# A two-block network on one core: the gating bias in two passes for both token blocks, and products of ones between bare attention steps

## What is computed

```python
def spatial_gating(h, w_in, ln_g, ln_b, w_s, b_s, w_out):
    u, v = jnp.split(jax.nn.gelu(h @ w_in), 2, axis=-1)          # 2048 wide each
    v = layer_norm(v, ln_g, ln_b)
    vg = v.reshape(B, nc, SG_CHUNK, SG_GROUPS, SG_WIDTH // SG_GROUPS)   # 2 blocks of 128 tokens, 8 groups
    mixed = jnp.einsum('gts,bcsgd->bctgd', w_s, vg) + b_s.T[None, None, :, :, None]
    return (u * mixed.reshape(B, L, SG_WIDTH)) @ w_out

def odd_mixer(x, w_in, q_norm_g, kv_norm_g, w_uq, w_ukv, w_o):
    out_c = dsa_attention(...)            # 8 heads, each token sees its 64 best-scored keys
    out_d = causal_block_attention(...)   # 8 heads
    return jnp.concatenate([out_c, out_d], axis=-1) @ w_o
```

## Time and profile before

| | |
|---|---|
| median of three runs | 2561.55 us |
| the profiled execution | 2558.21 us, its span 2556.4 us |
| mean granted TensorE clock | 0.968 |
| TensorE busy | 2424.2 us, 95% of the span |
| VectorE busy | 1718.7 us, 67% |
| ScalarE busy | 1191.6 us, 47% |
| DMA | 501 MB, 196 GB/s on average |

### The profile page before, as it was taken

How to read it: one execution, slowest core, us unless ns; L and a number is a source line. 1 busy time by engine, 2 the same in 40 slices (tenths; PEclk the granted TensorE clock), 3 DMA queues, 4 the chain that set the end, 5 groups by cost and what they waited for, 6 DMA issues and landing times.

```text
span 2556.4 us, 34122 instructions
## 1 busy us (share of the span) xinstructions
PE 2424.2 (95%) x14294; PEld 2078.5 (81%) x14294; DVE 1718.7 (67%) x2273; ACT 1191.6 (47%) x1523; POOL 98.9 (4%) x187
## 2 busy tenths in 40 slices
PE   7999999898989999999999999989999899899997
PEld 3778888667789999998899997767777777678776
DVE  5997776653766656655556655577887684678776
ACT  3222222333554544446344444465766644566665
POOL 0111111010000000000000000000000000000000
PEclk9999999999999999999899999999999996999999
DMA  6777787322124545465245542257887521388774
GB/s 274 231 238 263 264 265 252 132 79 94 67 100 167 184 178 179 168 224 191 105 149 177 189 174 102 99 184 271 335 323 293 211 94 53 138 309 329 295 289 175
DMA packets 80386, 501.16 MB, mean 196 GB/s; under 512 B 9605, under 2 KB 10709, under 8 KB 28497
## 3 DMA queue, kind: packets, MB, share of 16 engines
q1 hardware_dynamic: 59120, 423.66, 45.1%
q0 software_dynamic: 21088, 75.01, 9.2%
HBM read 497.58 MB, written 1.05 MB: 195 GB/s over the span
## 4 chain that ended last, share of the span: by engine, by line
PE 70%; DVE 16%; ACT 9%; issue 3%; DMA 2%; ACTq 0%; DVEq 0%; SPq 0%
PE bank L402 68%; DVE wl L1957 7%; ACT wh L1340 6%; DVE macc L1993 1%; ACT s L1438 1%; DVE f L2152 1%; PE bank L613 1%; DVE s L2143 1%; DVE rs L2017 1%; PE bank L1234 1%; DMA raw<-in_wstream 1%; DMA raw<-in_wmod 1%; DMA mring<-in_wmod 1%; DVE hl L2127 0%; ACT H L1447 0%
## 5 line engine op out<-in xcount | busy, mean ns | idle before, releaser
L1957 DVE TENSOR_TENSOR wl<-raw,wh 128x2048 fp32r<-128x2048 f32 (+1 forms) x432 | 903.8, 2097 | 410.7 <-ACT wh L1340 407.8
L1340 ACT ACTIVATE wh<-raw 128x2048 fp32r<-128x2048 f32 (+1 forms) x432 | 755.3, 1756 | 365.2 <-PE bank L402 349.3
L402 PE MATMUL bank<-hh,wh 128*128 128x258 f32 (+2 forms) x2200 | 696.6, 317 | 31.6 <-DVE wl L1957 7.7
L402 PE MATMUL bank<-hh,wl 128*128 128x258 f32 (+2 forms) x2200 | 676.8, 308 | 0.0
L402 PE MATMUL bank<-hl,wh 128*128 128x258 f32 (+2 forms) x2200 | 675.4, 307 | 0.0
L402 PEld LDWEIGHTS bank<-hh,wh 128*128 128x128 f32 x2200 | 424.2, 193 | 62.0 <-DVE hl L2127 8.1
L402 PEld LDWEIGHTS bank<-hl,wh 128*128 128x128 f32 x2200 | 424.8, 193 | 18.5
L402 PEld LDWEIGHTS bank<-hh,wl 128*128 128x128 f32 x2200 | 422.8, 192 | 18.9
L402 PE MATMUL bank<-wh,hh 128*128 128x512 f32 (+1 forms) x704 | 277.9, 395 | 5.5 <-DVE hl L2903 2.8
L402 PE MATMUL bank<-wh,hl 128*128 128x512 f32 (+1 forms) x704 | 273.4, 388 | 0.0
L402 PE MATMUL bank<-wl,hh 128*128 128x512 f32 (+1 forms) x704 | 273.3, 388 | 0.0
(11 more groups left out here) (437 smaller groups left out, 2678.1 us busy)
## 6 DMA issues: line engine op xcount, KB each, us to landing
raw<-in_wstream SPq DMA_DIRECT2D x393, 1024.0 KB, 4.9
mring<-in_wmod POOLq DMA_DIRECT2D x128, 512.0 KB, 4.6
raw<-in_wmod SPq DMA_DIRECT2D x6, 1024.0 KB, 7.1
X<-in_xT SPq DMA_DIRECT2D x1, 2048.0 KB, 12.4
mods<-in_wmod SPq DMA_DIRECT2D x2, 1024.0 KB, 18.9
bias<-in_nabias POOLq DMA_DIRECT2D x16, 128.0 KB, 2.5
c_sglg<-in_sglg POOLq DMA_DIRECT2D x1, 1024.0 KB, 4.5
c_sglb<-in_sglb POOLq DMA_DIRECT2D x1, 1024.0 KB, 6.6
```

The source lines that it names most:

```text
L402: return e.matmul(out, lhsT, rhs, start=start, stop=stop, skip_group_check=True)
L1340: e.activation(wh[i % NB][:, o], raw[i % NR][:, o], ACT.Copy).then_inc(*slab_high(st.split + m))
L1957: e.tensor_tensor(wl[i % NB][:, o], raw[i % NR][:, o], wh[i % NB][:, o].bitcast(F32), ALU.subtract).then_inc(*slab_low(st.split + m))
```

## The change

In `gating(m)` the bias comes first and is added for both token blocks at once: two fp32r products of one row, whose moving operand is the group's 128 biases repeated twice by a zero step, once with the high part `sg.bh` and once with the low part `sg.bl`. Then follow the two f32 products with `sg.ws`, accumulating. ScalarE writes `sg.bh` (1024 values in one partition) and `sg.one` (128 ones) before it evacuates the first quarter of v; VectorE writes `sg.bl` as the difference ahead of v's sums. `sg.bh` takes the place of `sg.tmp` in memory, which is dead by then.

A helper `fill(n, cols)` issues n f32 products of the 128x128 `ones` with `ones` to the bank that is next in turn, without claiming it; nobody reads the result. `fill(2, P)` comes behind each of the five bare steps and behind each `turned(i)`, seven times in all, 14 products of 128 columns.

```diff
@@ sg room @@
-        sg.tmp = sb(ph, "tmps", [P, 4, T])
+        with ExitStack() as pre:
+            sg.tmp = sb(pre, "tmps", [P, 4, T])
+        sg.bh = sb(ph, "sgbh", [1, 8 * P], F32R)
...
+        sg.bl = sb(ph, "sgbl", [1, 8 * P], F32R)
+        sg.one = sb(ph, "sgone", [1, P], F32R)
@@ TensorE @@
+        def fill(n, cols=T):
+            b = st.turn % 8
+            while b in st.kept:
+                b = (b + 1) % 8
+            if b in st.drain:
+                w.wait_ge(*st.drain[b])
+            w.wait_ge(dve_out, "ones")
+            out = banks[b][:, 0:cols].rearrange("p (a b) -> p a b", b=P)
+            for _ in range(n):
+                mm(out, ones[:], ones[:].unsqueeze(1).to_broadcast([P, cols // P, P]), True, True)
...
                 w.wait_ge(dve_out, "v norm")
                 w.wait_ge(const_in["sgws"], 0)
-                w.wait_ge(const_in["sgbs"], 0)
+                w.wait_ge(act_out, "sg one")
+                w.wait_ge(dve_out, "sg bias")
+                for t, first in ((sg.bh, True), (sg.bl, False)):
+                    mm(b[:, 0:T].rearrange("p (q t) -> p q t", q=2), sg.one[:], t[:, P * g:P * g + P].unsqueeze(1).to_broadcast([1, 2, P]),
+                       first, False)
                 for q in range(2):
-                    mm(b[:, P * q:P * q + P], sg.v[:, q, P * m:P * m + P], sg.ws[:, g, :], True, False)
-                    ins = mm(b[:, P * q:P * q + P], ones[0:1, :], sg.bs[:, P * g:P * g + P], False, True)
+                    ins = mm(b[:, P * q:P * q + P], sg.v[:, q, P * m:P * m + P], sg.ws[:, g, :], False, True)
...
-            attend(5)
+            for _ in range(5):
+                attend(1)
+                fill(2, P)
             for i in (2, 3):
                 turned(i, bank(("turn", "od", i), dve_out, "turn l", "od", i))
+                fill(2, P)
                 attend(1)
@@ ScalarE, quarter n of v @@
                 w.wait_ge(result, "sgv", n)
+                if n == 0:
+                    w.wait_ge(const_in["sgbs"], 0)
+                    e.activation(sg.bh[:], sg.bs[:], ACT.Copy).then_inc(*act_out("sg bias"))
+                    e.activation(sg.one[:], ones[0:1, :], ACT.Copy).then_inc(*act_out("sg one"))
@@ VectorE, layer_norms @@
                 mean, var = (sg.st[:, :, i] for i in (4, 5))
+                w.wait_ge(act_out, "sg bias")
+                e.tensor_tensor(sg.bl[:], sg.bs[:], sg.bh[:].bitcast(F32), ALU.subtract).then_inc(*dve_out("sg bias"))
```

## The result

The changed kernel took 2550.6 us (median of 22 executions, 2524.2 to 2593.0), the kernel before 2570.2 us (22 executions, 2551.2 to 2615.5). The ratio is 0.9908, 95% interval 0.9883 to 0.9933, so it is faster by 24 us (17 to 30). The prediction said 2526 and 2517 to 2546: the direction was right, the time lay 4.6 us above the range, and the gain was a third smaller than the 35.5 us forecast.

A forecast was written before the change was run, and what follows sets the result against it. TensorE's order of work was taken to bound the kernel. Gating 18.0 plus mixer 17.5 gave 35.5 us off the profiled 2558.2, so 2522.7; with 3.3 for the median of three runs, 2526 us, range 2517 to 2546.

The forecast's parts named there:

- 18.0 us forecast: Gating: shorter bias products and full clock in both blocks of four save 18.0 us, about 9 of it the clock.
- Rival C: Each gating's two bias products: the repeated operand is read slowly, at 1.2 us each; 2574 us, slower; chance 0.05.
- Rival A: Gating's blocks of four: the low clock stays once or twice, 4.6 us each; 2531 to 2535 us; chance 0.13.
- The mixer's sum: Second mixer: bare steps save 0.8 us and the stretch after them 16.7 us, together 17.5 us.
- The bare stretch: Second mixer's bare attention steps, 2108.51 to 2124.15: 15.6 us becomes 14.8 at full clock, fills included; saves 0.8.
- which one fill shortens to about 0.3: Second mixer, before 2119.16: one fill cuts TensorE's 0.78 us wait for Y to about 0.3 us.
- The stretch behind: Second mixer, 2124.15 to 2161.39: 37.2 us at half clock becomes 20.5 at full clock; saves 16.7 us.
- VectorE is busy only 14.9 us of those 37.2 and ScalarE 12.8 ... so both fit: Second mixer after the bare steps: both engines' busy times fit into the 20.5 us forecast there.
- Rival B: Second mixer: the clock falls despite the fills, about +4 us instead of -17.5; 2547 us; chance 0.11.
- For it ... one fall at any of the seven steps lasts to 2161: Second mixer, argument for Rival B: a single clock fall at any filled step keeps the clock low until 2161.
- Its own scatter is that of the three runs, 6 us each way: Whole kernel: the forecast time scatters 6 us each way, as the three runs of the kernel before did.
- I read the recurrence as evidence that such a mixture holds the clock: From 683.40 to 710.70, four-row and full-height f32 products kept 1.00 for 27.3 us; so new gating blocks likely would.

## Why the prediction was off

**The gating was right term by term.** 18.0 us forecast, 18.0 found, in all nine traces of the new form. A gating is 1.06 to 1.07 us against 1.07; VectorE's subtraction is 1.21 us against 1.2 and takes all of the slack, with 0.15 us of waiting on ScalarE and at most 0.1 us on v, where I took 0; ScalarE's two passes 1.35 against 1.4; the wait for z 0.37 against 0.3. Within it two prices offset each other: a one-row product with the repeated operand costs 0.20 us rather than 0.12, and seems to include the change of height that I had counted by itself (the two passes together 0.42 us, against 0.24 and one change of 0.19). Rival C, that such an operand is slow, is out. Rival A, that the low clock stays, is out: no new gating ever fell. In the one-row fills' trace TensorE was busy in 7.20 of 7.20 us and fell to 0.50. The Trainium skill, "TensorE: Matmul & The Clock Gate", section "Why this matters for your kernels", says that a TensorE kept busy without gaps keeps its clock; that trace disagrees.

**The mixer's sum was 3 us too high.** 17.5 us forecast, 14.5 in the best case, 1.5 short in each half. The bare stretch was to go from 15.6 to 14.8 us and became 16.3 (2091.57 to 2107.83), because a fill costs 0.60 us behind 64-column products (0.45 taken; the switch to other heights around it was left out), and because the two waits in it are 0.66 and 0.85 us where 0.3 was put. The step "which one fill shortens to about 0.3" failed: with the clock up, TensorE comes to Y sooner, and VectorE does not finish it sooner. In the two traces whose bare steps ran with fills at 0.50 there is no wait before Y's first turn. The stretch behind was to take 20.5 us and took about 22, 1.12 of it the next wait for Y. "VectorE is busy only 14.9 us of those 37.2 and ScalarE 12.8 ... so both fit" is the step there: a small busy share does not say that a result is ready when it is wanted. The prediction's list of what could go wrong had a wait for exp, not one for Y or hl, and the sum had no term for it.

**The mixer's clock was treated as certain or absent.** The forecast had one fall, at the bare steps, that the fills cure, and B had it stay. "For it ... one fall at any of the seven steps lasts to 2161" looked at the seven steps alone. The traces show a third thing: the bare steps hold under full-height fills, and the clock falls at another wait, behind Y (13.7 us in three of four traces of the changed kernel), behind hl, or 57 us ahead of the first fill. With three of four at 78.2 instead of 72.0 us this is an estimated 4.7 us of the mean. 35.5 - 3.0 - 4.7 gives 27.8, inside the measured 17 to 30. Rival B's 2547 is the nearest of the times forecast, by luck: it had the mixer gain nothing, and in the changed kernel's four traces the mixer gained 8.3 or 14.5 us.

**The base was too low, and its scatter too small.** "Its own scatter is that of the three runs, 6 us each way" is the step that failed here. The median of the kernel before beside the result was 2570.2, 8.6 above the 2561.55 of the three runs; the mean over the 86 is 2574.0, and single executions go 40 us further. Either miss alone would have left the time in the range: 2561.6 less the measured 24 is 2538, and 2570.2 less the forecast 35.5 is 2535. Together they put it outside. A base of 2574.0 less 27.8 is 2546; measured are medians around 2551, mean 2552.4. Three runs were few. But the trace itself could have warned: with 20 separate stretches at 0.50, and a recurrence that runs 4-row and 128-row products in turn and happened to stay at 1.00, much in one execution is chance. I read the recurrence as evidence that such a mixture holds the clock. In seven of twelve traces it didn't.

**What stays open.** The two traces lose 61 us at 0.50 between them (163 to 102), the means only 40 (206 to 166), and the difference of the means of the times is 21.6 (2.6) us, 6 less than the 27.8, more than two standard errors. The trace after was as much a favourable execution of its kernel as the first trace was of its own. Where the other executions have the rest of their low time can't be seen, since only profiled ones show it. One place is known: the mixer of the fills-alone trace, which has the same TensorE program there, took 102.3 us. Counted in, the five mixers with the seven fills are 9.8 us above 72.0 on average, and 35.5 - 3.0 - 9.8 is 22.7, within a standard error of the 21.6. With five traces that is a possible answer, not a shown one. Why the clock falls behind a wait in one execution and not in the next was not settled either: in the first two traces of the changed kernel TensorE did the same work with the same 1.12 us gap ahead. And the recurrence's fills took 20 us off the time at 0.50 and 3.3 us were added in its trace, yet the mean did not move; that is not explained.

## What to carry over

Mark the stretches at 0.50 in a trace and ask of each what TensorE did ahead of it: with few rows per product, busy was not enough here, and removing such products or adding full-height ones worked where they stand, while a later short wait may take the fall over. Ask also which stages at 1.00 have the same mixture, because they may fall in another execution; a time from three runs and one trace is then a small sample, and the range must hold that. Judge a stage by its own length in the trace (18.0 us came out exactly) and the kernel by many executions of both, in turn on one chip.

## What the hardware showed unexpectedly

- TensorE stayed at 0.50 with 71.70 of 71.70 and 58.00 of 58.00 us busy, and fell to it out of 7.20 of 7.20 us busy. In the first of these it came back at a turn of Y and a fill back to back; with fills of one row at the same place it did not.
- One-row fp32r products of 256 columns with an operand repeated by a zero step run at 0.20 to 0.22 us each; the repetition costs nothing that these rows show.
- Executions of one program differ by 65 us (2548 to 2614), and the time follows the time at 0.50 by 0.42 us per us; the stage lengths at a given clock repeat to 0.1 us.
